# Attention outputs of a pair of heads: one group of matmuls per pair, key block by key block

## The reference, cut to what matters

```
s = einsum('bqhd,bkhd->bhqk', q_blk, k) * scale      # mla: chunks, fox: decay
p = softmax(bias_mask(i, s), axis=-1)                # keys after the query's block: 0
out = einsum('bhqk,bkhd->bqhd', p, v)

sc = einsum('blhd,bmhd->bhlm', qc, kc) * scale + bias # band, in chunks of 64
pw = softmax(sc, axis=-1)
out = einsum('bhlm,bmhd->blhd', pw, vc)
```

## Time and profile before

| what | us |
|---|---|
| median of 3 runs | 2024.33 |
| lowest and highest run | 2023.63, 2025.32 |
| the profiled execution's own time | 2025.37 |
| its span, first to last instruction | 2023.2 |
| busy in the span: TensorE / VectorE / ScalarE | 1995.8 / 1137.5 / 814.5 |
| `mla` and `fox` attention in the span | about 150 to 231, tail to 244 |
| band attention in the span | about 1127 to 1159, tail to 1172 |

### The profile page before, as it was taken

One profiled execution on the slowest core, in us unless ns is written; L12 is line 12 of the kernel. 1 busy time (PEld: TensorE's weight loads), 2 busy tenths in 40 slices (PEclk: granted clock), 3 DMA queues, 4 the chain that ended last, 5 costly groups with the idle time before them and its releaser, 6 DMA issues.

```text
span 2023.2 us, 23761 instructions
## 1 busy us (share of the span) xinstructions
PE 1995.8 (99%) x9734; PEld 1647.9 (81%) x9734; DVE 1137.5 (56%) x1618; ACT 814.5 (40%) x1162; POOL 111.4 (6%) x120
## 2 busy tenths in 40 slices
PE   8999999999999999999999999999999999999998
PEld 7887788878888888888888687888888888888886
DVE  6857657576544675366368878733435444234346
ACT  5647633456323333133342535532333333123145
POOL 0004300221000000000010400000000000000000
PEclk9999999999999999999999999999999999999999
DMA  4320023212423332332333132222322233232232
GB/s 134 107 82 22 22 84 93 95 63 63 146 88 100 84 104 98 90 104 83 104 125 105 42 94 84 84 94 94 104 91 97 84 104 100 88 114 95 93 105 83
DMA packets 164442, 184.45 MB, mean 91 GB/s; under 512 B 6760, under 2 KB 125799, under 8 KB 164335
## 3 DMA queue, kind: packets, MB, share of 16 engines
q1 hardware_dynamic: 161006, 175.03, 27.2%
q10 hardware_dynamic: 2624, 5.78, 0.8%
q0 software_dynamic: 704, 2.13, 0.3%
HBM read 180.81 MB, written 2.12 MB: 90 GB/s over the span
## 4 chain that ended last, share of the span: by engine, by line
PE 95%; DVE 2%; ACT 1%; issue 1%; DMA 0%; POOL 0%; DVEq 0%; SPq 0%; ACTq 0%; POOLq 0%
PE ps L453 29%; PE ps L455 29%; PE ps L454 29%; PE ps L596 2%; PE ps L610 1%; PE ps L583 1%; PE ps L644 1%; PE ps L833 1%; DMA W<-in_w_in_dram 0%; ACT HH L1382 0%; DVE arena L2094 0%; PE ps L821 0%; DVE HL L2014 0%; PE ps L755 0%; PE ps L567 0%
## 5 line engine op out<-in xcount | busy, mean ns | idle before, releaser
L1897 DVE TENSOR_TENSOR WL<-W,WH 128x2048 fp32r<-128x2048 f32 (+2 forms) x162 | 367.5, 2270 | 352.6 <-ACT WH L1332 352.3
L453 PE MATMUL ps<-HH,WH 128*128 128x512 f32 (+1 forms) x1464 | 560.2, 383 | 2.9 <-DVE HL L2014 2.9
L455 PE MATMUL ps<-HH,WL 128*128 128x512 f32 (+1 forms) x1464 | 557.2, 381 | 0.0
L454 PE MATMUL ps<-HL,WH 128*128 128x512 f32 (+1 forms) x1464 | 557.2, 381 | 0.0
L1332 ACT ACTIVATE WH<-W 128x2048 fp32r<-128x2048 f32 (+2 forms) x163 | 307.2, 1886 | 278.9 <-DMA W<-in_w_ff_dram 115.3
L453 PEld LDWEIGHTS ps<-HH,WH 128*128 128x128 f32 x1464 | 276.2, 189 | 57.0 <-issue 2.6
L455 PEld LDWEIGHTS ps<-HH,WL 128*128 128x128 f32 x1464 | 276.1, 189 | 52.3
L454 PEld LDWEIGHTS ps<-HL,WH 128*128 128x128 f32 x1464 | 276.3, 189 | 51.7 <-issue 0.2
L453 PE MATMUL ps<-WH,arena_r 128*128 128x512 f32 (+1 forms) x616 | 238.5, 387 | 0.0
L455 PE MATMUL ps<-WH,arena_r 128*128 128x512 f32 (+1 forms) x616 | 238.5, 387 | 0.0
L454 PE MATMUL ps<-WL,arena_r 128*128 128x512 f32 (+1 forms) x616 | 238.4, 387 | 0.0
(11 more groups left out here) (376 smaller groups left out, 2276.9 us busy)
## 6 DMA issues: line engine op xcount, KB each, us to landing
W<-in_w_in_dram SPq DMA_DIRECT2D x50, 1024.0 KB, 5.1
W<-in_w_ff_dram SPq DMA_DIRECT2D x32, 1024.0 KB, 5.2
W<-in_ffn_w_up_dram SPq DMA_DIRECT2D x44, 512.0 KB, 4.9
W<-in_w_gate_dram SPq DMA_DIRECT2D x16, 1024.0 KB, 5.0
W<-in_ffn_w_down_dram SPq DMA_DIRECT2D x10, 1024.0 KB, 5.0
W<-in_w_out_dram SPq DMA_DIRECT2D x8, 1024.0 KB, 5.0
W<-in_w_branch_dram SPq DMA_DIRECT2D x8, 1024.0 KB, 5.0
W<-in_w_br_ssm_dram SPq DMA_DIRECT2D x4, 1024.0 KB, 5.0
```

The costliest lines, as they stand in the source:

```text
L453: pe.matmul(out_, st[0], mv[0], start=first, stop=False)
L454: pe.matmul(out_, st[0], mv[1], start=False, stop=False)
L455: return pe.matmul(out_, st[1], mv[0], start=False, stop=last)
L1897: dve.tensor_tensor(WL[:, j % RING, 0:n], W[:, j % RING, 0:n], plain(WH[:, j % RING, 0:n]), ALU.subtract).then_inc(slab_lo, 1)
```

## The change

The outputs are made once per pair, not once per tile. For each key block kb and head one matmul takes the values of kb as before, but moves all queries from tile kb to tile 3: 512, 384, 256 and 128 columns, 8 matmuls per pair. The columns of a later key block are added in the same bank. For this the transposed weights of a key block have to lie side by side over all tiles: each head gets 5 rows of 384 numbers, in which tile t, key block kb stands at 384*kb + 128*t (`turned_tiles` is where a tile is written, `turned_row` where a key block is read). `heads_pt` and `band_pt` move accordingly, and fox's causal mask goes to another place of the arena, 4096.

The group of a pair is issued on PE in the last step of the next pair, between that step's scores and turns; it waits for all copies of its pair. `pairs_out` counts pairs. A copy waits until the group of the pair before is done.

```diff
+        def turned_tiles(pts, t):
+            return pts[:, :, 0:t + 1, P * t:P * t + P] if t < 3 else pts[:, :, 1:5, 0:P]
+        def turned_row(pts, odd, kb):
+            return pts[:, odd].rearrange("p k c -> p (k c)")[:, 4 * P * kb:3 * P * kb + 4 * P]
...
         def heads_pt():
-            a, b = at(11840, 768), at(23552, 1792)
-            return by_tile(a[:, 0:256], a[:, 256:768], b[:, 0:768], b[:, 768:1792])
+            v = arena[:, 1152:25600].rearrange("p (o x) -> p o x", o=2)
+            return v[:, :, 10176:12096].rearrange("p o (k c) -> p o k c", c=3 * P)
...
                 def outputs(step):
                     tag, j, pair, t = step_of(tags, step)
-                    if t == 0:
-                        outs[0] = bank((tag, "O", pair), counted=False, pinned=PAIR_BANK)
-                    o = outs[0]
-                    taken(pe, (tag, "PT", turned(2 * j + 1)))
-                    if t >= 2:
-                        taken(pe, (tag, "PT", 2 * j))
-                    for kb in range(t + 1):
+                    o = bank((tag, "O", pair), counted=False, pinned=PAIR_BANK)
+                    for r in range(2 * (j - t), 2 * j + 2):
+                        taken(pe, (tag, "PT", turned(r)))
+                    for kb in range(NT):
                         for odd in range(2):
                             h = 2 * pair + odd
-                            mm = pe.matmul(o[HD * odd:HD * odd + HD, t * P:(t + 1) * P],
-                                           v(tag)[:, kb, h * HD:(h + 1) * HD],
-                                           turned_weights(pts, 2 * j + odd)[:, kb * P:(kb + 1) * P],
-                                           start=(kb == 0), stop=(kb == t))
+                            mm = pe.matmul(o[HD * odd:HD * odd + HD, kb * P:NT * P], v(tag)[:, kb, h * HD:(h + 1) * HD],
+                                           turned_row(pts, odd, kb), start=(kb == 0), stop=(kb == NT - 1))
                     mm.then_inc(pairs_out, 1)
 
                 for step in range(steps):
                     scores(step)
+                    if step >= NT and step % NT == NT - 1:
+                        outputs(step - NT)
                     if step >= LAG:
                         turns(step - LAG)
-                    if step >= LAG + 2 and step % 2 == 1:
-                        outputs(step - LAG - 2)
-                        outputs(step - LAG - 1)
...
                     if t == 0:
                         turns(steps - 2)
-                        outputs(steps - 4)
-                        outputs(steps - 3)
                     if t == 1:
                         turns(steps - 1)
                     if t == 2:
-                        outputs(steps - 2)
                         outputs(steps - 1)
...
-                            act.wait_ge(pairs_out, first + step - 3)
+                            act.wait_ge(pairs_out, (first + step) // NT)
...
-                            dve.wait_ge(pairs_out, first + step - 3)
-                        freed(dve.tensor_copy(pts[t], b[:, 0:2 * (t + 1) * P]), (tag, "PT", 2 * j))
+                            dve.wait_ge(pairs_out, (first + step) // NT)
+                        freed(dve.tensor_copy(turned_tiles(pts, t), b[:, 0:2 * (t + 1) * P].rearrange(
+                            "p (o k c) -> p o k c", o=2, c=P)), (tag, "PT", 2 * j))
...
-                    dve.wait_ge(pairs_out, first + step + 1)
+                    dve.wait_ge(pairs_out, (first + step) // NT + 1)
```

More of the change, by code:

```diff
@@ L304, in weights @@
             return p[s // 2 % NT][:, s % 2 * n:s % 2 * n + n]
-        def turned_weights(pts, s):
-            return weights(pts, s)
+        def turned_tiles(pts, t):
+            return pts[:, :, 0:t + 1, P * t:P * t + P] if t < 3 else pts[:, :, 1:5, 0:P]
+        def turned_row(pts, odd, kb):
+            return pts[:, odd].rearrange("p k c -> p (k c)")[:, 4 * P * kb:3 * P * kb + 4 * P]
         def step_of(tags, step):
@@ L334, in band_pt @@
         def band_pt():
-            q = at(0, 2560)
-            return by_tile(q[:, 0:256], q[:, 256:768], q[:, 768:1536], q[:, 1536:2560])
+            return at(0, 2, 5, 3 * P)
         def krows(name):
@@ L1216, in pool_heads @@
             def pool_heads():
-                causal = at(11328, S)
+                causal = at(4096, S)
                 use(pool, ("mla", "KT", HEADS - 1))
@@ L1424, in attention @@
                         if step >= 4:
-                            act.wait_ge(pairs_out, first + step - 3)
+                            act.wait_ge(pairs_out, (first + step) // NT)
                         for r in (2 * j, 2 * j + 1):
                             b = use(act, (tag, "PT", r))
-                            freed(act.activation(turned_weights(pts, r), b[:, 0:(t + 1) * P], ACT.Copy), (tag, "PT", r))
+                            freed(act.activation(turned_tiles(pts, t)[:, r % 2],
+                                                 b[:, 0:(t + 1) * P].rearrange("p (k c) -> p k c", c=P), ACT.Copy),
+                                  (tag, "PT", r))
                     if beside_scores is not None:
@@ L2210, in dve_mla @@
                 dve.wait_ge(mask_ready, 2)
-                masks = {"mla": mask, "fox": at(11328, S)}
+                masks = {"mla": mask, "fox": at(4096, S)}
                 def beside_scores(step):
```

1 line of the change is left out of this document (removed).

## The result

| | median us (runs) | lowest to highest | profiled execution, span |
|---|---|---|---|
| before, same comparison | 2024.82 (4) | 2023.63 to 2025.32 | 2025.37, 2023.2 |
| changed | 2034.27 (4) | 2033.01 to 2035.74 | 2033.01, 2030.8 |
| changed, a second series | 2034.03 (5) | 2032.09 to 2035.88 | span 2031.9 |
| before, beside the second series | 2025.75 (8) | 2024.46 to 2026.43 | |

The changed kernel takes 1.0047 times the time of before, 95% interval 1.0035 to 1.0059; the second series gives 1.0041 (1.0027 to 1.0055). It is slower by 9.5 us in the first series, 8.3 in the second, 7.6 between the spans of the two profiled executions. Forecast were 6.2 us more and 2030.5 us.

What follows compares the result with a forecast made beforehand. TensorE was taken to bound the kernel, with VectorE close behind in the attention stretches. Terms -1.5 (first branch), +3.6 (second branch), +3.7 (band) and +0.4 (ends) gave +6.2 us, hence 2030.5 us; range 2026 to 2036.

Steps and rivals of the forecast that it cites:

- the clock case: Rival: an idle gap of 2.9 us in the band halves TensorE's clock for one or two pairs, 2036 to 2041; chance 0.05.
- first branch, first group: First output group of the first attention branch starts at about 164.2 against 165.35, as TensorE is earlier: -1.15 us.
- second branch, three periods: Three pair periods of the second attention branch take 33.4 us in all against 29.84 before: +3.6 us.
- to the next stage: From an attention loop's last group to the next stage's matmuls takes 3.0 us against 2.09: +0.9 us each.
- tail of that stage: The last pair's group, standing between the next stage's matmuls, takes 2.5 us against 2.9 for two old ones: -0.4 us each.
- band, two periods: Two pair periods of the band attention, 10.31 and 11.06 us, take 21.37 in all against 17.64: +3.7 us.
- The closed loop: In attention, group, VectorE's copies and scores, and ScalarE's t = 3 copies wait in a ring: 9.79 us per period; chance 0.64.
- TensorE's gain: One output group of 2.30 us replaces two: 0.30 us less per pair, 3.6 over 12 pairs, and 2.6 of waits go.
- the rival in which TensorE is the only limit: ScalarE and VectorE keep up in both attention stretches, so only TensorE's gain counts: -6.2 us, 2018.1 us; chance 0.09.
- The overhead per matmul: In the output groups, a skill rule of about 60 cycles per matmul would give 3.6 us more; rejected from the trace.
- Two heads side by side over 512 columns: Rival: the odd head starts a pass late, each output group 0.43 us longer, +5.2 us on top, 2035.7; chance 0.08.
- The waits: VectorE waits about 1.9 us at t = 0's copy; TensorE before groups about 2 in second branch, 2.1 to 2.9 in band.

Runs made afterwards that it cites:

- the opened version: Before's kernel with one group of 20 narrow matmuls per pair behind the transposes, waits tile by tile, a second place for turned tile t = 0: 2021.05 us.
- with fillers: The changed kernel plus 8 matmuls on constants ahead of the group's waits, first three pairs of second branch and band: 2033.19 us.

## Why the prediction was right or wrong

The sign, the mechanism and the places were right, and 2034.27 lies in the range, near its top. The range was said to leave out the clock case, and the measured time has falls of the clock in it. That it lies in the range even so is luck in part: the falls came, but each was small. The working of the forecast beside the profiled executions, in us against before (start-to-start times from the earlier trace rows and the timeline above):

| term | forecast | measured |
|---|---|---|
| first branch, first group | -1.15 | -1.42 |
| first branch, three periods | -1.5 | -1.30 |
| second branch, three periods | +3.6 | +5.04, of it 1.04 clock |
| to the next stage | +0.9 | +0.85 |
| tail of that stage | -0.4 | -0.47 |
| band, first group | +0.56 | +0.58 |
| band, two periods | +3.7 | +4.09 |
| to the next stage | +0.9 | +0.62 |
| tail | -0.4 | -0.39 |
| sum | +6.2 | +7.60 |

The start of the first group is only good to about 1 us (162.59 to 163.93 in the profiles with the group at this place and all its waits ahead), because the stage ahead of the attention scatters. Counted from the attention's first matmul it is firm: 14.06 us in all four of these profiles, against 15.15 before (150.20 to 165.35). That is -1.09 us, against -1.15 forecast; the other -0.33 of the first row is scatter. For "to the next stage" after the band and the tail ahead of it, before has

```profile
1158.73 0.47 PE L453 MATMUL ps<-WH,HH 128*128 128x512 f32 x1
```

which is 2.31 us behind its last group, against 2.93 us in the changed kernel. The forecast took 2.09 for both ends; with 2.31 this term would have been +0.69. The tails are what the lag loses over them: 234.26 - 231.09 = 3.17 behind the second branch, 2.70 where the band's attention starts, 1166.72 - 1158.73 = 7.99 behind the band, and 7.60 in the span.

- **The closed loop.** Right. The second branch's periods were forecast as 11.35, 10.98 and 11.06; they are 11.39, 11.06 and, with fillers and so at full clock, 11.35. In the band 10.31 and 11.06 were forecast, 10.58 and 11.15 measured. Moving the waits, which opens the loop and changes nothing else, took 11.1 us away, so the wait ahead of the group is shown as the cause and not only added up; 6.8 us of the 9.9 between the profiles are the loop itself, the rest slow groups. Not tested is the whole group issued later, when its one wait is over.
- **TensorE's gain.** Right: 2.30 us per group. It is worth what was said where nothing waits: the opened version is at 9.08 and 9.10 us per period in the second branch, and ends 4.5 us under before, against the 6.2 of the rival in which TensorE is the only limit.
- **The overhead per matmul.** The trace was right to go by. 24 instructions less per pair save 0.02 or 0.03 us, not the 0.3 us that 12 matmuls would give by an estimate from the 60 cycles each of the Trainium skill (TensorEngine Tiling (Array Packing), Instruction Overhead).
- **Two heads side by side over 512 columns.** The rival fell: groups take 2.31 us, not 2.73.
- **The waits.** VectorE's were forecast as about 1.9 us each and are 2.1 in the mean of seven in the first stretch and 2.7 in the band. TensorE's were forecast as about 2 us, in the band 2.1 to 2.9; they are 1.50 to 2.02 in both. My gap of 2.9 us was too long because TensorE's own part was taken too small: it is busy for 8.55 of 10.58 and 9.25 of 11.15 us in the band's two periods, not for 8.2, and is idle for 2.03 and 1.90.
- **The clock: the step that failed.** I gave "the clock falls" 0.05, with one condition (the single gap of 2.9 us in the band) and one price (5.3 us for a pair wholly at half clock). Both were wrong. The falls came behind waits of 1.50 to 2.02 us, in the second branch too, and a mean clock of 0.996 or 0.997 in eight of the nine runs suggests at least one in most executions; and one fall takes 3.4 us at half clock and costs 1.0 to 1.6 us (a group takes 3.41 to 3.98 instead of 2.37). As a term that belongs in the sum it was about +1.8 us in the median, by the estimate above; with it the sum is +8.0, against 8.3 and 9.5 measured in the two series. The Trainium skill (TensorE: Matmul & The Clock Gate, HAM oscillation) lays such falls to idle gaps between bursts. The runs agree in kind: the falls stood behind waits, and with the gaps filled the profile has none. I had used it as a rival of one lump instead of as a small cost with a high chance.
- **What is left** is 0.3 us of the one series and 1.5 of the other. Part of it is the loop, whose periods came out 0.04 to 0.29 us longer than forecast; and the three runs of before that the forecast started from (2024.33) were low, 27 later ones give 2025.15. Of the 1.2 us between the two series 0.9 come from before: its median is 2024.82 of four runs in the first and 2025.75 of eight in the second. Its executions are of two kinds: of the 27, twelve have a mean clock of 0.999 and a median of 2023.97, fifteen 0.998 and 2025.85. That fits one more stretch at half clock in the latter, but none of them was profiled.

## What to carry to other kernels

Before merging small groups of matmuls into one, write down what its first instruction must wait for and what stands behind it in the queue: one wait ahead of the whole group made the last copy hold up 60% of work that was ready, and all that came after. Keep the waits at the piece that needs them, put the group behind what the other engines need next, and give the first tile that is overwritten a second place; the three together turned +9 us into -4.5, whatever the width of the matmuls. And cost an idle gap on TensorE at its length plus a chance of a fall of the clock behind it, here 1.0 to 1.6 us each.

## What the runs showed of the hardware

- The number of float32 matmul instructions hardly matters at this size: 40 of 128 columns take 2.40 us, 16 of 128 to 512 columns 2.37 or 2.38, with 64-column weights of two heads side by side.
- After waits of 1.50 to 2.02 us once per 11 us, the granted clock fell to 0.50 for 3.4 us, once or twice in each of three profiles, not always at the same output group. With matmuls on constants in these waits the one profile has no such fall.
- The granted clock also fell to 0.50 for some 3.4 us near 60 us, with TensorE never idle, shortly after 16 matmuls of one moving column each, in four of eleven profiles.
